# Order of the U and V gathers in the expert stage of a decoder layer: blocks of 16 in place of alternation

## The chip, the cores and the metric

The kernel runs on one core of a Trainium2 chip. The metric is the device time of one execution in microseconds (us), less is better; the numbers given are medians of runs. The profile is one execution taken by the hardware profiler. Its engines: PE (TensorE, matrix multiply), DVE (VectorE), ACT (ScalarE), POOL (GpSimd) and SP (SyncE), each with its own in-order instruction stream, and 16 DMA engines that move data between HBM and on-chip memory.

## What is computed

A decoder layer for 256 tokens of width 2048 in float32: attention and short convolution, output projection, LayerNorm, then product-key experts (PEER), LayerNorm. The change touches only the experts:

```python
def _peer(h, w_query, sub_keys, expert_u, expert_v):
    ...
    eid = i1 * N_KEYS + i2                    # 16 experts of 16384 per token and head
    g = jax.nn.softmax(best_s, axis=-1).astype(h.dtype)
    ...
    def chunk(args):
        hx, e, gw = args
        a = jax.nn.gelu(jnp.einsum('td,thkd->thk', hx, expert_u[e]))
        return jnp.einsum('thk,thkd->td', gw * a, expert_v[e])
```

There are 8 heads and 16 experts a head. Each expert is one row of 2048 floats in `expert_u` and one in `expert_v`, so every token needs 128 rows of each: 256 x 128 x 2 rows of 8 KB, 512 MiB in all.

## The kernel before

The first third, up to about 634 us, is projections, attention and the query scores. The expert stage follows. It is cut into 16 units (`NU`): unit n is one head for one tile of 128 tokens (units 0 to 7 are tile 0, 8 to 15 tile 1). A unit has 16 expert places k (`TOPK`). For each (n, k) there is one U gather and one V gather: an indirect DMA that POOL issues and that fetches 128 rows (one for each token of the tile) of 8 KB, 1 MiB in all. U(n,k) and V(n,k) stand for them below; m = 16n + k.

- POOL (L351 to L377) issues all gathers from one in-order stream. `gather_u` waits at k = 0 for the ids of the unit (`ids_ok`), and always for a free place in the ring of 8 U tiles (`RU`): `dots_done` of m - 8. `gather_v` waits for a free place in the ring of 8 V tiles (`RV`): `v_used` of m - 8. All gathers go to one DMA queue. At the start all of U(0,.) is issued; then the loop over n pairs U(n+1,k) with V(n,k).
- DVE (from L1251) makes `ids(0)`, the top-k that gives `eid`. Then for each unit it does 16 times `dot(n,k)` (L1217), which multiplies a U tile with the token tile `xh` and sums along the row. Behind dot 0 of a unit stands `gates_of(n-1)` (L1220), behind dot 1 `ids(n+1)` (L1163 to L1210), and behind dot 2 of unit 9 `take(0)` (L1229), which adds the finished sum of tile 0 to `xh` and takes its statistics; it waits until all 128 V tiles of tile 0 are used.
- ACT turns the 16 dots of a unit into Gelu values (L865) and, once the gates are there, writes 16 diagonal matrices 128x128 (L872) in one of two halves of `diag`.
- PE (L625) multiplies each diagonal with the V tile (four products of 128x512, each of which is two rows in the profile: 8 rows a V tile), summing a whole token tile's 128 experts in four PSUM banks. Its V tiles come in the order of m. It waits for `diag_ok` at the start of a unit, for the landing of each V tile, and before unit 8 for `acc_taken` of `take(0)`.
- SP loads the two rows of the last LayerNorm once all ids are there, and stores the output.

The order of the work is written by hand; no scheduler moves it.

Of the kernel before, what the change touches and what calls it, by code (L numbers as in the profile page):

```python
# [29 lines left out]
TOPK = 16  # L30
# [22 lines left out]
def build(nc, x, w_in, cmp_k_pos, cmp_k_w1, cmp_k_b1, cmp_k_w2, cmp_v_pos, cmp_v_w1, cmp_v_b1, cmp_v_w2,  # L53
# [248 lines left out]
    def _(pool):  # L302
# [48 lines left out]
        def gather_u(n, k):  # L351

            m = TOPK * n + k
            if k == 0:
                pool.wait_ge(S["ids_ok"], n + 1)
            if m >= RU:
                pool.wait_ge(S["dots_done"], m - RU + 1)
            nc.gpsimd.indirect_dma_start(out=u_slot[m % RU][:, :], out_offset=None, in_=expert_u[0],  # L358
                                         in_offset=bass.IndirectOffsetOnAxis(ap=eid[:, n, k:k + 1], axis=0)
                                         ).then_inc(s_u[m % RU], 16)  # L360

        def gather_v(n, k):

            m = TOPK * n + k
            if m >= RV:
                pool.wait_ge(S["v_used"], m - RV + 1)
            nc.gpsimd.indirect_dma_start(out=v_slot[m % RV][:, :], out_offset=None, in_=expert_v[0],  # L367
                                         in_offset=bass.IndirectOffsetOnAxis(ap=eid[:, n, k:k + 1], axis=0)
                                         ).then_inc(s_v[m % RV], 16)
# [3 lines left out]
        for n in range(NU):  # L373
            for k in range(TOPK):
                if n + 1 < NU:
                    gather_u(n + 1, k)
                gather_v(n, k)  # L377


# [913 lines left out]
```

## Time and profile before

| what | value |
|---|---|
| median of 3 runs | 1963.75 us (1963.17 to 1964.27) |
| the profiled execution, whole | 1962.15 us |
| its span | 1960.4 us |
| expert stage | about 634 to 1946 us |
| PE busy over the span | 1548.9 us, 79% |
| DVE busy | 1092.1 us, 56% |
| POOL busy | 700.9 us, 36% |
| HBM traffic | 328 GB/s over the span, 421 in the expert stage |

How to read it: the page cuts the span into 40 slices of 49 us and gives for each the busy share in tenths, the granted clock of PE (1.00 is 2.4 GHz, 0.50 is 1.2 GHz), the mean share of the 16 DMA engines and what they moved. A window row has first the window and its length, then the busy time and the number of instructions of PE, PE's weight loads, DVE, ACT and POOL, and at its end the granted clock, the DMA share and GB/s. A row of the timeline has start, duration, engine, line, operation and operands, and in brackets how long the engine was idle before it and what ended that. A row of the chain has start, duration and what the time went to.

### The profile page before, as it was taken

Reading aid. Unit: us, or ns where it says so; the run is one execution under the profiler, and the core shown is the slowest. Engines: PE = TensorE matmul, PEld = TensorE weight load, DVE = VectorE, ACT = ScalarE, POOL = GpSimd, SP = SyncE. Lnnn points to the kernel's source line nnn. Section 1 sums busy time; section 2 is a strip of 40 time slices with the busy share of each in tenths; the row PEclk is TensorE's granted clock in tenths of the full one; section 3 lists DMA queues with packets and bytes.
Section 4 is the critical chain, followed back from the end, with each engine's and each line's share of the span. In section 5 each row is a group of like instructions: output and inputs, shape, how many; then the busy total and the mean of one; then the engine's idle time right before and its main releaser. Section 6 shows DMA issues by size and latency. Waiting matters only on the chain.

```text
span 1960.4 us, 18229 instructions
## 1 busy us (share of the span) xinstructions
PE 1548.9 (79%) x6469; PEld 935.4 (48%) x6469; DVE 1092.1 (56%) x1775; ACT 446.0 (23%) x918; POOL 700.9 (36%) x562
## 2 busy tenths in 40 slices
PE   6999999999897077776877767775877687776886
PEld 6679989989897033232322323322333232232333
DVE  3666656655744866465564655647646466454432
ACT  3655465464443011011010110101101001010010
POOL 1100000000000784554655546554555554545420
PEclk8899999999898589989999999997999999989999
DMA  9555444445541999999999999999999999999992
GB/s 305 204 193 153 145 135 152 147 133 178 163 155 47 416 421 421 422 422 422 422 421 422 422 422 422 421 422 422 421 422 421 421 422 421 422 422 421 422 407 104
DMA packets 172979, 644.59 MB, mean 329 GB/s; under 512 B 13310, under 2 KB 100454, under 8 KB 106856
## 3 DMA queue, kind: packets, MB, share of 16 engines
q0 software_dynamic: 78640, 556.83, 68.8%
q1 hardware_dynamic: 90976, 85.99, 14.0%
q10 hardware_dynamic: 3288, 0.78, 0.2%
q8 instruction: 46, 0.75, 0.2%
q14 instruction: 29, 0.24, 0.0%
HBM read 641.46 MB, written 2.10 MB: 328 GB/s over the span
## 4 chain that ended last, share of the span: by engine, by line
DMA 49%; PE 37%; POOL 5%; DVE 4%; issue 2%; ACT 1%; DVEq 1%; ACTq 1%; POOLq 0%
DMA v_slot<-in_expert_v_dram,eid 41%; PE psum_all L404 21%; PE psum_all L625 9%; DMA u_slot<-in_expert_u_dram,eid 8%; POOL u_slot L358 3%; POOL v_slot L367 2%; PE psum_all L520 1%; DVE u_slot L1217 1%; PE psum_all L456 1%; PE psum_all L457 1%; PE psum_all L458 1%; ACT diag L872 1%; DVE w_lo L902 1%; PE psum_all L594 0%; ACTq L645 0%
## 5 line engine op out<-in xcount | busy, mean ns | idle before, releaser
L625 PE MATMUL psum_all<-v_slot,diag 128*128 128x512 f32 x2048 | 959.9, 620 | 361.8 <-DMA v_slot<-in_expert_v_dram,eid 188.4
L1217 DVE SCALAR_TENSOR_TENSOR u_slot<-u_slot,xh 128x2048 f32<-128x2048 f32 x256 | 583.4, 2291 | 518.6 <-DMA u_slot<-in_expert_u_dram,eid 518.4
L625 PEld LDWEIGHTS psum_all<-v_slot,diag 128*128 128x128 f32 x2048 | 388.5, 197 | 932.6 <-issue 448.5
L367 POOL DMA_INDIRECT v_slot<-in_expert_v_dram,eid x256 | 386.6, 1510 | 514.8 <-PE psum_all L625 478.2
L358 POOL DMA_INDIRECT u_slot<-in_expert_u_dram,eid x256 | 295.9, 1156 | 212.5 <-DVE eid L1210 124.5
L902 DVE TENSOR_TENSOR w_lo<-w_ring,w_hi 128x512 fp32r<-128x512 f32 x304 | 205.8, 690 | 176.1 <-ACT w_hi L656 173.5
L404 PE MATMUL psum_all<-act_hi,w_hi 128*128 128x256 f32 x896 | 260.6, 291 | 14.5 <-DVE w_lo L902 13.6
L404 PE MATMUL psum_all<-act_hi,w_lo 128*128 128x256 f32 x896 | 256.0, 286 | 0.0
L404 PE MATMUL psum_all<-act_lo,w_hi 128*128 128x256 f32 x896 | 256.0, 286 | 0.0
L656 ACT ACTIVATE w_hi<-w_ring 128x512 fp32r<-128x512 f32 x304 | 189.0, 629 | 184.4 <-PE psum_all L404 184.2
L865 ACT ACTIVATE u_act<-u_dot 128x16 f32<-128x16 f32 x16 | 3.4, 215 | 932.0 <-DVE u_slot L1217 932.0
L404 PEld LDWEIGHTS psum_all<-act_hi,w_hi 128*128 128x128 f32 x896 | 174.7, 195 | 19.0 <-DVE act_lo L907 10.3
L404 PEld LDWEIGHTS psum_all<-act_lo,w_hi 128*128 128x128 f32 x896 | 174.8, 195 | 0.5 <-issue 0.5
L404 PEld LDWEIGHTS psum_all<-act_hi,w_lo 128*128 128x128 f32 x896 | 174.4, 195 | 0.0
L349 POOL DMA_DIRECT2D skeys<-in_sub_keys_dram x1 | 1.2, 1172 | 393.9 <-PE psum_all L404 393.9
L872 ACT ACTIVATE diag<-ident,gate 128x128 f32<-128x128 f32 x256 | 76.5, 387 | 75.3 <-DVE gate L1226 75.3
L404 PE MATMUL psum_all<-w_hi,mix_hi 128*128 128x256 f32 x256 | 74.0, 289 | 0.0
L404 PE MATMUL psum_all<-w_lo,mix_hi 128*128 128x256 f32 x256 | 73.4, 287 | 0.0
L404 PE MATMUL psum_all<-w_hi,mix_lo 128*128 128x256 f32 x256 | 73.3, 286 | 0.0
L404 PEld LDWEIGHTS psum_all<-w_hi,mix_hi 128*128 128x128 f32 x256 | 50.1, 196 | 0.7 <-issue 0.7
L404 PEld LDWEIGHTS psum_all<-w_lo,mix_hi 128*128 128x128 f32 x256 | 50.1, 196 | 0.3 <-issue 0.3
L404 PEld LDWEIGHTS psum_all<-w_hi,mix_lo 128*128 128x128 f32 x256 | 50.1, 196 | 0.0
(201 smaller groups left out, 969.3 us busy)
## 6 DMA issues: line engine op xcount, KB each, us to landing
w_ring<-in_w_in_dram SPq DMA_DIRECT2D x88, 512.0 KB, 4.7
w_ring<-in_w_out_dram SPq DMA_DIRECT2D x32, 512.0 KB, 4.5
w_ring<-in_w_query_dram SPq DMA_DIRECT2D x32, 512.0 KB, 4.5
w_ring<-in_cmp_k_w_dram POOLq DMA_DIRECT2D x8, 1024.0 KB, 7.1
w_ring<-in_cmp_v_w_dram POOLq DMA_DIRECT2D x8, 1024.0 KB, 5.7
u_slot<-in_expert_u_dram,eid POOLq DMA_INDIRECT x256, 36.3
v_slot<-in_expert_v_dram,eid POOLq DMA_INDIRECT x256, 35.7
xh<-in_x_dram SPq DMA_DIRECT2D x4, 512.0 KB, 7.4
```

The lines of the kernel that those rows point to most:

```text
L358: nc.gpsimd.indirect_dma_start(out=u_slot[m % RU][:, :], out_offset=None, in_=expert_u[0], in_offset=bass.IndirectOffsetOnAxis(ap=eid[:, n ...
L367: nc.gpsimd.indirect_dma_start(out=v_slot[m % RV][:, :], out_offset=None, in_=expert_v[0], in_offset=bass.IndirectOffsetOnAxis(ap=eid[:, n ...
L404: ins = nc.tensor.matmul(o, st, mv, start=(k == 0 and b == 0 and n == 0), stop=(k == KC - 1 and n == 2), skip_group_check=True)
L456: nc.tensor.matmul(o, blk_hi[:, kv, j, :], w_hi[:, q % 4, :], start=(j == 0), stop=False)
L457: nc.tensor.matmul(o, blk_hi[:, kv, j, :], w_lo[:, q % 4, :], start=False, stop=False)
L458: nc.tensor.matmul(o, blk_lo[:, kv, j, :], w_hi[:, q % 4, :], start=False, stop=False).then_inc(S["slot_used"], 1)
L520: ins = nc.tensor.matmul(bank[6][:, 128 * t:128 * t + 128], vv, pp, start=(n == 0), stop=(n == len(parts) - 1))
L625: ins = nc.tensor.matmul(bank[4 + q][:, :], diag[:, n % 2, k, :], v_slot[m % RV][:, 512 * q:512 * q + 512], start=m % (TOPK * PH) == 0, st ...
L656: nc.scalar.activation(w_hi[:, q % 4, :], src, ACT.Copy).then_inc(S["hi_done"], 1)
L872: ins = nc.scalar.activation(diag[:, n % 2, k, :], ident[:, :], ACT.Copy, scale=gate[:, n, k:k + 1])
L902: V.tensor_tensor(w_lo[:, q % 4, :], src, w_hi[:, q % 4, :].bitcast(F32), ALU.subtract).then_inc(S["lo_done"], 1)
L1217: V.scalar_tensor_tensor(u_slot[m % RU][:, :], u_slot[m % RU][:, :], 1.0, xh[:, n // PH, :], ALU.mult, ALU.mult, accum_out=u_dot[:, n, k:k ...
```

## The change

In the loop over units POOL issued U(n+1,k) and V(n,k) in turn. Now it issues the 16 U gathers of unit n+1 first and then the 16 V gathers of unit n. Waits, rings and slots stay as they were, and so does every other engine's program.

```diff
         for n in range(NU):
             for k in range(TOPK):
                 if n + 1 < NU:
                     gather_u(n + 1, k)
+            for k in range(TOPK):
                 gather_v(n, k)
```

On POOL, where the gathers of V(0,.) end and those of U(2,.) begin, the program stands so before; `u_slot0` with both waits is U(2,0), the V rows ahead of it are V(0,12) to V(0,15):

```order
L358 DMA u_slot4_143<-in_expert_u_dram,eid_126 128x2048 [waits dots_done]
L367 DMA v_slot4_151<-in_expert_v_dram,eid_126 128x2048 [waits v_used]
L358 DMA u_slot5_144<-in_expert_u_dram,eid_126 128x2048 [waits dots_done]
L367 DMA v_slot5_152<-in_expert_v_dram,eid_126 128x2048 [waits v_used]
L358 DMA u_slot6_145<-in_expert_u_dram,eid_126 128x2048 [waits dots_done]
L367 DMA v_slot6_153<-in_expert_v_dram,eid_126 128x2048 [waits v_used]
L358 DMA u_slot7_146<-in_expert_u_dram,eid_126 128x2048 [waits dots_done]
L367 DMA v_slot7_154<-in_expert_v_dram,eid_126 128x2048 [waits v_used]
L358 DMA u_slot0_139<-in_expert_u_dram,eid_126 128x2048 [waits dots_done,ids_ok]
L367 DMA v_slot0_147<-in_expert_v_dram,eid_126 128x2048 [waits v_used]
```

The same engine and place after:

```order
L367 DMA v_slot4_151<-in_expert_v_dram,eid_126 128x2048 [waits v_used]
L367 DMA v_slot5_152<-in_expert_v_dram,eid_126 128x2048 [waits v_used]
L367 DMA v_slot6_153<-in_expert_v_dram,eid_126 128x2048 [waits v_used]
L367 DMA v_slot7_154<-in_expert_v_dram,eid_126 128x2048 [waits v_used]
L358 DMA u_slot0_139<-in_expert_u_dram,eid_126 128x2048 [waits dots_done,ids_ok]
L358 DMA u_slot1_140<-in_expert_u_dram,eid_126 128x2048 [waits dots_done]
L358 DMA u_slot2_141<-in_expert_u_dram,eid_126 128x2048 [waits dots_done]
L358 DMA u_slot3_142<-in_expert_u_dram,eid_126 128x2048 [waits dots_done]
L358 DMA u_slot4_143<-in_expert_u_dram,eid_126 128x2048 [waits dots_done]
L358 DMA u_slot5_144<-in_expert_u_dram,eid_126 128x2048 [waits dots_done]
```

All of U(1,.) has moved ahead of V(0,.), and each wait for `v_used` now stands ahead of 16 U gathers instead of one.

On POOL at the end of the U gathers, before (the last U here is U(15,15), beside it V(14,15), and V(15,.) follows):

```order
L358 DMA u_slot6_145<-in_expert_u_dram,eid_126 128x2048 [waits dots_done]
L367 DMA v_slot6_153<-in_expert_v_dram,eid_126 128x2048 [waits v_used]
L358 DMA u_slot7_146<-in_expert_u_dram,eid_126 128x2048 [waits dots_done]
L367 DMA v_slot7_154<-in_expert_v_dram,eid_126 128x2048 [waits v_used]
L367 DMA v_slot0_147<-in_expert_v_dram,eid_126 128x2048 [waits v_used]
L367 DMA v_slot1_148<-in_expert_v_dram,eid_126 128x2048 [waits v_used]
L367 DMA v_slot2_149<-in_expert_v_dram,eid_126 128x2048 [waits v_used]
```

The same end of U(15,.) after:

```order
L358 DMA u_slot4_143<-in_expert_u_dram,eid_126 128x2048 [waits dots_done]
L358 DMA u_slot5_144<-in_expert_u_dram,eid_126 128x2048 [waits dots_done]
L358 DMA u_slot6_145<-in_expert_u_dram,eid_126 128x2048 [waits dots_done]
L358 DMA u_slot7_146<-in_expert_u_dram,eid_126 128x2048 [waits dots_done]
L367 DMA v_slot0_147<-in_expert_v_dram,eid_126 128x2048 [waits v_used]
L367 DMA v_slot1_148<-in_expert_v_dram,eid_126 128x2048 [waits v_used]
L367 DMA v_slot2_149<-in_expert_v_dram,eid_126 128x2048 [waits v_used]
L367 DMA v_slot3_150<-in_expert_v_dram,eid_126 128x2048 [waits v_used]
```

Behind the last U gather 32 V gathers are left, where 17 were.

## Rows read from the trace of the kernel before

**Rows 1.** The page: DMA share and GB/s in 40 slices; the chain by line.
```profile
DMA  9555444445541999999999999999999999999992
GB/s 305 204 193 153 145 135 152 147 133 178 163 155 47 416 421 421 422 422 422 422 421 422 422 422 422 421 422 422 421 422 421 421 422 421 422 422 421 422 407 104
...
DMA v_slot<-in_expert_v_dram,eid 41%; PE psum_all L404 21%; PE psum_all L625 9%; DMA u_slot<-in_expert_u_dram,eid 8%; POOL u_slot L358 3%; POOL v_slot L367 2%; PE psum_all L520 1%; DVE u_slot L1217 1%; PE psum_all L456 1%; PE psum_all L457 1%; PE psum_all L458 1%; ACT diag L872 1%; DVE w_lo L902 1%; PE psum_all L594 0%; ACTq L645 0%
```

**Rows 2.** Window row of one unit (columns as told above).
```profile
1158.60:1239.00 80.40, 60.16 (x128) 24.04 (x128) 45.03 (x69) 7.91 (x21) 42.19 (x33) 0.96 1.01 421
```

**Rows 3.** Timeline in the steady part of a unit: DVE, POOL, PE, POOL.
```profile
1146.28 2.29 DVE L1217 SCALAR_TENSOR_TENSOR u_slot<-u_slot,xh 128x2048 f32<-128x2048 f32 x1 [2.66 <-DMA u_slot<-in_expert_u_dram,eid]
...
1147.78 1.59 POOL L367 DMA_INDIRECT v_slot<-in_expert_v_dram,eid  x1 [2.12 <-PE psum_all L625]
...
1148.78 3.70 PE L625 MATMUL psum_all<-v_slot,diag 128*128 128x512 f32 x8 [1.28 <-DMA v_slot<-in_expert_v_dram,eid]
...
1149.68 0.94 POOL L358 DMA_INDIRECT u_slot<-in_expert_u_dram,eid  x1 [0.30 <-issue]
...
1151.24 2.29 DVE L1217 SCALAR_TENSOR_TENSOR u_slot<-u_slot,xh 128x2048 f32<-128x2048 f32 x1 [2.67 <-DMA u_slot<-in_expert_u_dram,eid]
```

**Rows 4.** Timeline of ACT: the Gelu row of unit 1 and of unit 15.
```profile
759.50 0.22 ACT L865 ACTIVATE u_act<-u_dot 128x16 f32<-128x16 f32 x1 [57.69 <-DVE u_slot L1217]
...
1885.01 0.21 ACT L865 ACTIVATE u_act<-u_dot 128x16 f32<-128x16 f32 x1 [69.31 <-DVE u_slot L1217]
```

**Rows 5.** The page's DMA issues: count, median us from issue to landing.
```profile
u_slot<-in_expert_u_dram,eid POOLq DMA_INDIRECT x256, 36.3
```

**Rows 6.** The chain of the last 80 us.
```profile
1882.67 2.31 DVE u_slot L1217 x2
...
1885.61 4.79 ACT diag L872 x16
...
1890.44 55.22 PE psum_all L625 x128
```

**Rows 7.** Startup gathers issued at 634.2, 635.5, 648.1 and 657.3: time to landing.
```profile
DMA to landing us min/median/max: 5.4/5.4/5.4
...
DMA to landing us min/median/max: 7.9/7.9/7.9
...
DMA to landing us min/median/max: 15.2/15.2/15.2
...
DMA to landing us min/median/max: 8.5/8.5/8.5
```

**Rows 8.** Timeline of DVE: first row of unit 1's top-k, dot 2 behind it.
```profile
690.87 0.48 DVE L1168 MAX8 t_val<-scores 128x8 f32<-128x128 f32 x2
...
699.99 2.29 DVE L1217 SCALAR_TENSOR_TENSOR u_slot<-u_slot,xh 128x2048 f32<-128x2048 f32 x1
```

**Rows 9.** Timeline of POOL while DVE does dots back to back.
```profile
669.18 1.91 POOL L358 DMA_INDIRECT u_slot<-in_expert_u_dram,eid  x1 [0.30 <-issue]
```

**Rows 10.** Window rows of the startup's U stream.
```profile
650.00:670.00 20.00, 0.00 (x0) 0.00 (x0) 19.41 (x28) 1.68 (x3) 11.20 (x6) 0.50 1.01 413
...
660.00:670.00 10.00, 0.00 (x0) 0.00 (x0) 10.00 (x9) 0.00 (x0) 8.47 (x6) 0.50 1.00 400
...
670.00:672.00 2.00, 0.00 (x0) 0.00 (x0) 2.00 (x3) 0.00 (x0) 1.70 (x2) 0.50 1.04 430
```

**Rows 11.** Timeline of DVE: `take(0)` from its first row to the dot behind it.
```profile
1340.68 2.48 DVE L1234 SCALAR_TENSOR_TENSOR xh<-xh,psum_all 128x512 f32<-128x512 f32 x4
...
1346.17 2.29 DVE L1217 SCALAR_TENSOR_TENSOR u_slot<-u_slot,xh 128x2048 f32<-128x2048 f32 x1
```

**Rows 12.** PE's clock behind idle time: window rows, and PE's row at 1343.
```profile
1168.70:1172.50 3.80, 3.76 (x5) 1.69 (x6) 3.43 (x20) 1.28 (x1) 0.00 (x0) 0.50 1.01 423
...
1343.26 50.02 PE L625 MATMUL psum_all<-v_slot,diag 128*128 128x512 f32 x112 [19.79 <-DVE xh L1234]
...
1347.00:1352.00 5.00, 5.00 (x13) 2.18 (x12) 5.00 (x5) 0.00 (x0) 2.78 (x2) 1.00 1.01 421
```

## Prediction

> **What bounds the kernel now.** I read the slices and the chain of the page first [rows 1]. From slice 14 on (about 637 us) the DMA digit is 9 and 421 to 422 GB/s flow in every slice until the last two. That is the expert stage: 512 gathers of 1 MiB. The chain is mostly `v_slot` and `u_slot` DMA. One unit (16 U and 16 V gathers) takes 80.4 us, DMA share 1.01, and in it PE is busy 60.2 us, DVE 45.0 and POOL 42.2 [rows 2]: three engines with room, and DMA with none. U gathers are 4.97 us apart in the steady part [rows 3], so a gather of either kind costs 2.49 us of DMA; over all units it is (1885.01 - 759.50)/14 = 80.4 us a unit [rows 4], 80.0 without the two LayerNorm rows, which take about 5 us of DMA once. In [rows 3] DVE waits 2.67 us for each U, PE 1.26 us for each V, and POOL for PE: about 14 gathers stand in the DMA queue, which is why one takes 36 us to land [rows 5]. Nothing but the rate of DMA sets the unit. The end is different [rows 6]: after the last U gather (landed 1882.67) come its dots, the gates, 4.79 us of diagonals, and then 55.2 us in which PE works through unit 15's 16 V tiles, 3.45 us each, while DMA runs dry; then 14.7 us of final LayerNorm and store to the span's 1960.4.
>
> **What the change moves.** No instruction is added or removed; POOL's 480 paired gathers are put in blocks, with the same waits. The total of DMA work is the same 512 x 2.49 us. What can change is whether the queue ever runs empty, and what is left for after its end.
>
> Term 1, the end. Before, U(15,15) is gather number 16 + 14x32 + 31 = 495 in POOL's order. After, all U of unit 15 come first, then V(14) and V(15): V(14,0) is number 16 + 14x32 + 16 + 1 = 481. If DMA never idles it lands 14 x 2.49 = 34.9 us before 1882.67, at 1847.8. From there PE has 32 V tiles in one run, as V comes at 2.49 us and PE needs 3.45: 2.1 us of slow start (below) + 32 x 3.45 = 112.5 us, to 1960.3, where it now ends at 1945.65. That is **+14.7 us**, and certain as long as DMA sets the pace before it: in the alternating order half of that PE work lay under U transfers. The gates of unit 15 (5 us of diagonals) leave the path; that is inside the sum.
>
> Term 2, the steady unit. Does a block order keep DMA full? Follow POOL from the issue of V(n-1,15), t = 0. U(n+1,0) is issued 0.94 + 0.30 us later [rows 3]; behind one other gather it lands 7.9 us after its issue [rows 7]: t = 9.1. DVE then does dot 0 (2.21, the pitch of back-to-back dots [rows 9]), the gates (0.75, an estimate for two small instructions) and dot 1 (2.21) and starts the top-k of the next unit, from 690.87 to 699.99 = 9.1 us [rows 8]: 23.4. No further U slot comes free in that time. Six more dots at 2.21 (13.3) free the slot of U(n+1,15): 36.7. While dots run back to back POOL issues one gather per dot, 1.91 + 0.30 = 2.21 us [rows 9], so U(.,15) and V(n,0) are out at 41.1. DMA by then has 18 gathers to do since t = 0: V(n,0) lands near 18 x 2.49 + 2.9 = 47.7 (2.9 = 5.4 for a lone gather [rows 7] less its own 2.49). PE has been idle some 20 us and starts slow; then 8 V tiles (2.1 + 8 x 3.45 = 29.7) must be used before V(n,15) may be issued: t = 77.4. The unit of DMA is 80.0, so this loop fits with 2.6 us to spare, one gather's worth. Likeliest is therefore no loss, but a margin of 3% replaces a queue of 14 gathers.
>
> The tighter spot inside the unit is the top-k. The first ten U are in flight when it starts; the eleventh waits for dot 2, 2.21+0.75+2.21+9.1+2.21+0.35 = 16.8 us after U(.,0) landed, and the ninth further gather lands 9 x 2.49 = 22.4 us after it. An issue of up to 2.74 us under a dot and 4.4 us from there to landing end at 24.0 against the 24.9 us at which an unbroken stream would deliver it: 0.9 us to spare. The startup of the present trace is this very case, since its first 16 gathers are U alone. The tenth, issued at 648.1, landed at 663.3; the eleventh, issued at 657.3, at 665.8 [rows 7]: 2.5 us later, so no gap; and DMA moved 413 GB/s between 650 and 670 [rows 10] against 421 in a steady unit [rows 2] (2% less). By the first number the cost is nothing, by the second 2% of the 40 us of U in each unit, 0.8 us, over 14 units 11 us. I take 0.2 us a unit, **+3 us** (bounds 0 and +11), nearer to the landing times, since the sequel has V gathers left in the queue which the startup had not.
>
> The Trainium skill (SBUF — State Buffer, the paragraph on DVE blocking software-generated DMA) says GpSimd can be locked out by a DVE instruction and the DMA engines then sit idle for want of descriptors. Taken whole, it would idle DMA for much of each block of 16 dots (35 us a unit, 490 us in all); the trace shows the lockout only as the 2.21 us pitch, and DMA busy through it, so the sum takes nothing for it. The skill (DMA: Bandwidth & Descriptors, Anatomy of one DMA) fits 2.0 us + bytes/436 GB/s, 4.4 us for 1 MiB; the lone gather here took 5.4 with its issue. With 4.4 the loop would end at 76.4 in place of 77.4 and change nothing.
>
> Term 3, two places where DVE is late. At the start DVE runs behind (its first top-k stands in unit 0's dots), so unit 1's top-k at 690.87 to 699.99 falls when only U(1,0..9) may be out. U(1,0) landed at 681.1, U(1,9) would by 703.5; U(1,10) waits for dot 2, is issued at 702.5 and lands some 7.9 later, 710.4, where an unbroken stream has 706.0. Now V gathers fill this hole. **+3 us** (2 to 4.4). And `take(0)` stands behind dot 2 of unit 9: 1340.68 to 1346.17, 5.5 us of DVE [rows 11], plus up to 2 us in which it waits for V(7)'s last tile. Now 14 queued gathers hide it; after, it is in the loop above, where it meets 1 to 2.6 us of room: **+4.5 us** (3 to 6.5).
>
> Term 4, PE's clock. PE falls to a granted 0.50 in idle time and stays there 3.8 us after it starts [rows 12]: a matmul, 3.45/8 = 0.43 us at full clock, takes twice that, and about 2.1 us are lost. This happens once a unit now (6.3 us idle) and once a unit after (idle 80 - 57 = 23 us); the start after 19.8 us of idle is no longer than after 6.3. It is in the loop already.
>
> Sum: 14.7 + 3 + 3 + 4.5 = **+25 us**. On the profiled span of 1960.4 that is 1985.6. The execution profiled took 1962.15 in all, and the median of the three is 1963.75; I add to the median: **1989 us**, 1.3% slower.
>
> **Rivals.**
> - *Stretched unit.* The 2.6 us margin is not there, say because queued gathers land later than I take it or PE's slow start lasts twice as long (4.2 us): each unit is then 2 to 4.5 us over 80. For it: two spots with under 3 us to spare, and 400 GB/s between 660 and 670 in the startup's U stream [rows 10]. Against: the landing times. Price: 14 x 2 to 14 x 4.5 on top of 25: 2017 to 2052, middle about 2030.
> - *Shallow queue is slower.* DMA needs more than some 2 gathers in flight for its rate. With those 400 GB/s instead of 421, the 1245 us stream grows 5%, 62 us: 2051.
> - *Not slower.* A stream from one table goes faster than one that alternates. The startup's U stream has moments of 430 GB/s (670 to 672) [rows 10]; if the blocks held that, 2.1% of 1245 us = 26 us come back: 1963, and it decides from there: only above 430 GB/s is the kernel faster. Against: the 20 us around it have 413. The skill (DMA: Bandwidth & Descriptors) gives a ceiling of about 436 GB/s, which would be 3.5%, 44 us, and a time near 1945; no row here sustains it.
> - *No block in effect.* If rings kept U and V in lockstep anyway, nothing would change (1964). They can't: POOL is in order, and V(n,0) stands behind U(n+1,15).
>
> **Chances.** Forecast (DMA-bound units, +12 to +40): 0.66. Stretched unit: 0.20. Slower shallow queue, or several of these together (over +70): 0.06. Not slower or in effect nothing: 0.08, of it 0.03 faster by over 0.2%. 0.2% (4 us) is about what a measurement of this kernel can tell from no change. The range must hold 8 in 10: it begins at term 1 alone less 3 us, +12, and reaches into the stretched unit, 3.5 us a unit, +66: 1976 to 2030.
>
> **What would show it.** After: units of 80 us still, by the distance of the Gelu rows; DMA at 9 in all slices of the stage, with a dip near 705 and 1350; PE in runs of about 57 us with some 23 us between; the last PE run about 112 us, starting near 1858. Diagonals no longer end PE's idle time; the first V of a block does. Landing of gathers falls from 36 to some 10 us. Units of 82 us or more, or DMA slices of 7 and 8, would show the margin gone; under 80 us, a faster stream. I am wrong in kind if PE's last run stays near 55 us.

## The result and the profile after

The changed kernel takes **1992.49 us** (median of 4 runs, 1991.3 to 1993.92) against 1963.46 us of the kernel before in the same measurement: ratio 1.0152, 95% interval 1.0135 to 1.017, so 29 us slower. The forecast was 1989 us, the range 1976 to 2030. The profiled execution has a span of 1989.7 us, 29.3 more than before.

The page after, with the same two rows of slices and the same row of the chain as [rows 1], and the gathers' time to landing as in [rows 5]:

```profile
DMA  9555445445452999999999999999999999999992
GB/s 301 203 189 164 134 138 164 135 141 185 141 169 92 421 374 411 422 420 421 416 419 412 417 414 419 414 422 368 422 421 415 421 421 410 422 421 413 422 342 102
...
PE psum_all L626 26%; PE psum_all L405 21%; POOL u_slot L358 9%; DMA v_slot<-in_expert_v_dram,eid 8%; DVE u_slot L1218 6%; DMA u_slot<-in_expert_u_dram,eid 6%; POOL v_slot L367 1%; PE psum_all L521 1%; PE psum_all L457 1%; PE psum_all L459 1%; PE psum_all L458 1%; DVE w_lo L903 1%; DVE eq L1201 1%; DVE b_id L1209 1%; DVE t_idx L1179 0%
...
u_slot<-in_expert_u_dram,eid POOLq DMA_INDIRECT x256, 12.9
v_slot<-in_expert_v_dram,eid POOLq DMA_INDIRECT x256, 10.7
```

The line numbers from L380 on are one higher than before. Read the two rows of slices together. The DMA digit is 9 in every slice of the stage, as before; by it alone nothing happened. The GB/s row shows what did: 374 in slice 15, 368 in slice 28, 410 to 419 in many others where before stood 421 and 422, and 342 in the last but one, where before stood 407. The chain has turned over. Where DMA of `v_slot` held 41%, it now holds 8%, and the product of PE (L626) went from 9 to 26%. Gathers land after 11 to 13 us where they took 36: the queue that hid everything is short.

PE's runs after, from its timeline: the V tiles of unit 0, of unit 6, of units 7 and 8 (between them `take(0)`), of unit 13, and of 14 and 15 in one:

```profile
726.12 56.94 PE L626 MATMUL psum_all<-v_slot,diag 128*128 128x512 f32 x128 [102.13 <-DMA v_slot<-in_expert_v_dram,eid]
...
1209.36 57.66 PE L626 MATMUL psum_all<-v_slot,diag 128*128 128x512 f32 x128 [23.28 <-DMA v_slot<-in_expert_v_dram,eid]
...
1289.97 56.61 PE L626 MATMUL psum_all<-v_slot,diag 128*128 128x512 f32 x128 [22.95 <-DMA v_slot<-in_expert_v_dram,eid]
1375.38 56.58 PE L626 MATMUL psum_all<-v_slot,diag 128*128 128x512 f32 x128 [28.80 <-DMA v_slot<-in_expert_v_dram,eid]
...
1782.49 57.81 PE L626 MATMUL psum_all<-v_slot,diag 128*128 128x512 f32 x128 [27.72 <-DMA v_slot<-in_expert_v_dram,eid]
1863.41 111.55 PE L626 MATMUL psum_all<-v_slot,diag 128*128 128x512 f32 x256 [23.11 <-DMA v_slot<-in_expert_v_dram,eid]
```

A unit's 16 V tiles are one unbroken run of 57 us behind 23 us of idle time, and the diagonals no longer end that idle time. The last row is term 1 of the prediction: 256 rows, 32 tiles, 111.55 us, where [rows 6] had 128 rows and 55.22.

The windows of the three other places, after. The columns are those of [rows 2]; the last three are granted clock, DMA share, GB/s.

```profile
704.00:714.00 10.00, 0.00 (x0) 0.00 (x0) 10.00 (x11) 0.00 (x0) 8.72 (x5) 0.50 0.82 301
1173.00:1213.00 40.00, 16.72 (x36) 7.12 (x35) 39.04 (x64) 6.53 (x17) 24.79 (x14) 0.72 1.00 407
1300.00:1360.00 60.00, 46.59 (x109) 20.33 (x107) 28.23 (x59) 7.75 (x20) 20.63 (x20) 0.92 0.93 383
```

The same windows before:

```profile
704.00:714.00 10.00, 10.00 (x25) 4.38 (x24) 6.59 (x7) 0.00 (x0) 8.48 (x6) 1.00 1.02 423
1173.00:1213.00 40.00, 33.64 (x76) 13.47 (x74) 23.30 (x30) 1.68 (x3) 24.54 (x18) 1.00 1.01 422
1300.00:1360.00 60.00, 35.11 (x75) 14.46 (x76) 40.78 (x70) 7.96 (x21) 23.94 (x17) 0.83 1.01 422
```

The first is the hole of the start, the third that of `take(0)`, and the second the dip behind the top-k of an ordinary unit. There the DMA share is 1.00 (1.01 before) while 4% fewer bytes come. The strip of DMA over 1133 to 1213, 2 us a column, shows where in the unit:

```profile
GB/s 410 426 418 426 426 422 426 414 426 414 426 422 426 422 422 422 406 434 414 434 418 414 422 418 422 418 426 397 307 401 348 356 426 414 438 414 442 410 442 410
```

Columns 28 to 32 (1187 to 1197 us) fall to 307 to 401. The top-k of this unit ran from 1173.95 to 1182.9, and the next U gather behind it was issued at 1185.48. The same strip over 1293 to 1373, with `take(0)` in it, falls to nothing:

```profile
GB/s 430 410 434 418 422 422 422 430 406 434 414 434 410 426 426 410 438 406 430 414 430 410 418 434 410 434 414 426 414 381 74 0 94 414 406 393 320 377 422 426
```

### The profile page after: what moved, and what is told of

The parts are those of the page before. It is cut to its first block, busy times and chain, and to the rows that moved or that the text cites. A ratio compares the mean times of both kernels' runs of the same rounds, so it can differ in the third digit from the quotient of the medians.

```text
span 1989.7 us, 18229 instructions
## 1 busy us (share of the span) xinstructions
PE 1501.4 (75%) x6469; PEld 945.9 (48%) x6469; DVE 1077.1 (54%) x1775; ACT 445.8 (22%) x918; POOL 746.3 (38%) x562
## 4 chain that ended last, share of the span: by engine, by line
PE 53%; DMA 14%; DVE 14%; POOL 11%; issue 5%; DVEq 2%; ACT 1%; ACTq 1%; POOLq 0%
PE psum_all L626 26%; PE psum_all L405 21%; POOL u_slot L358 9%; DMA v_slot<-in_expert_v_dram,eid 8%; DVE u_slot L1218 6%; DMA u_slot<-in_expert_u_dram,eid 6%; POOL v_slot L367 1%; PE psum_all L521 1%; PE psum_all L457 1%; PE psum_all L459 1%; PE psum_all L458 1%; DVE w_lo L903 1%; DVE eq L1201 1%; DVE b_id L1209 1%; DVE t_idx L1179 0%
## 5 line engine op out<-in xcount | busy, mean ns | idle before, releaser
L626 PE MATMUL psum_all<-v_slot,diag 128*128 128x512 f32 x2048 | 912.7, 609 | 438.3 <-DMA v_slot<-in_expert_v_dram,eid 438.3
L626 PEld LDWEIGHTS psum_all<-v_slot,diag 128*128 128x128 f32 x2048 | 399.7, 196 | 950.6 <-issue 950.6
L1218 DVE SCALAR_TENSOR_TENSOR u_slot<-u_slot,xh 128x2048 f32<-128x2048 f32 x256 | 571.2, 2286 | 510.6 <-DMA u_slot<-in_expert_u_dram,eid 510.4
L358 POOL DMA_INDIRECT u_slot<-in_expert_u_dram,eid x256 | 383.4, 1498 | 372.5 <-DVE u_slot L1218 171.8
L367 POOL DMA_INDIRECT v_slot<-in_expert_v_dram,eid x256 | 344.5, 1346 | 339.3 <-PE psum_all L626 284.3
L405 PE MATMUL psum_all<-act_hi,w_hi 128*128 128x256 f32 x896 | 260.8, 291 | 14.7 <-DVE w_lo L903 12.2
L1235 DVE SCALAR_TENSOR_TENSOR xh<-xh,psum_all 128x512 f32<-128x512 f32 x8 | 5.0, 681 | 105.9 <-PE psum_all L626 105.9
```

The costliest lines, as they stand in the source:

```text
L405: ins = nc.tensor.matmul(o, st, mv, start=(k == 0 and b == 0 and n == 0), stop=(k == KC - 1 and n == 2), skip_group_check=True)
L626: ins = nc.tensor.matmul(bank[4 + q][:, :], diag[:, n % 2, k, :], v_slot[m % RV][:, 512 * q:512 * q + 512], start=m % (TOPK * PH) == 0, st ...
L1218: V.scalar_tensor_tensor(u_slot[m % RU][:, :], u_slot[m % RU][:, :], 1.0, xh[:, n // PH, :], ALU.mult, ALU.mult, accum_out=u_dot[:, n, k:k ...
```

## The experiments

Each run is compared with the kernel before in the same measurement. That kernel's median was 1963.46 us when the change was measured and 1959.99, 1962.51 and 1960.79 in the three later measurements, so a difference between two kernels that were not measured together can be off by up to 3.5 us; where it matters, the difference of the two losses, each against its own kernel before, stands beside it ("by the losses"). In the texts of expectation "theory" and "rival" are the two readings that the run is to tell apart. The first theory ("end and holes") is the prediction's: the loss is a longer end and three kinds of holes in which DVE is late. Its rival: a stream in blocks is slower as such, by a short queue or by reading one table at a time.

### Undoing the end, and the end alone

The lines that are new against the changed kernel (the four in the middle stand as there, further in):

```diff
+            if n + 1 < NU - 1:           # first run; in the second: if n + 1 == NU - 1
                 for k in range(TOPK):
                     gather_u(n + 1, k)
                 for k in range(TOPK):
                     gather_v(n, k)
+            else:
+                for k in range(TOPK):
+                    if n + 1 < NU:
+                        gather_u(n + 1, k)
+                    gather_v(n, k)
```

> The changed kernel with the last pair alone, U(15) with V(14), put back into alternation; units before it stay in blocks. Theory 'end and holes': the last U gather is number 495 of the order again, so PE's last run is 55 us and the 14.7 us of term 1 go: 1992.5 - 14.7 = 1978 us. Rival 'slower stream' (the loss is spread over all block units because a stream in blocks moves fewer GB/s): one unit of 15 is mended, about 2 us: 1990 us.

Measured: 1976.73 us against 1959.99, ratio 1.0076 (1.0059 to 1.0093).

> The kernel before with the last pair alone, U(15) and V(14), in blocks. Theory 'end and holes': only term 1, 1963.5 + 14.7 = 1978 us, last PE run about 112 us, units of 80.0 us up to there. Rival 'slower stream': one unit of 15, 1965 us.

Measured: 1974.26 us against 1959.99, ratio 1.0074 (1.0053 to 1.0095), +14.3 us for one reordered pair. Its last PE run:

```profile
1846.40 111.85 PE L631 MATMUL psum_all<-v_slot,diag 128*128 128x512 f32 x256 [38.62 <-DMA v_slot<-in_expert_v_dram,eid]
```

Term 1 said 14.7 us. It is there when only the last pair is in blocks, and it goes when only the last pair is put back: the median falls by 15.8 us, and the loss against the kernel before of each measurement from 29.0 to 16.7, by 12.3. A rate of the stream would have given 2 us in either.

### Moving DVE's long pieces behind dot 8

```diff
-                if k == 1 and n + 1 < NU:
+                if k == 8 and n + 1 < NU:
                     ids(n + 1)
-                if k == 2 and n == PH + 1:
+                if k == 8 and n == PH + 1:
                     take(0)
```

The last U gather of a block waits for dot 7, so behind dot 8 neither piece holds up a gather.

> The changed kernel with the top-k of the next unit behind dot 8 in place of dot 1, and take(0) behind dot 8 of unit 9 in place of dot 2; all U gathers of a block can then be issued without waiting for either. Theory 'end and holes': the dips of DMA behind the top-k, the hole at 704 to 714 us and the hole of take(0) go, 14 to 15 us; the end stays: 1978 us, units of 80.0 us. Rival 'slower stream' (some 10 gathers in flight in place of 14, or one table at a time, is what costs): nothing depends on DVE's order: 1990 to 1992 us.

Measured: 1977.76 us against 1959.99, ratio 1.0085 (1.0066 to 1.0103), 14.7 us less than the changed kernel (11.3 by the losses, 29.0 and 17.8). The profiled spans, 1989.7 and 1975.2, differ by 14.5. The same three windows:

```profile
704.00:714.00 10.00, 0.00 (x0) 0.00 (x0) 9.38 (x33) 0.00 (x0) 7.87 (x8) 0.50 1.01 422
1173.00:1213.00 40.00, 17.29 (x34) 7.28 (x33) 33.32 (x59) 1.90 (x4) 20.77 (x15) 0.70 1.01 422
1300.00:1360.00 60.00, 39.26 (x92) 17.10 (x90) 35.31 (x65) 7.75 (x20) 35.96 (x28) 0.86 1.01 420
```

301, 407 and 383 GB/s have become 422, 422 and 420. Over whole slices small dips are left (410 to 422). The U gathers still come in blocks of 16 from one table.

> Blocks in units 0 to 13, last pair in alternation, and top-k and take(0) behind dot 8: both edits of the two runs beside it together. Theory 'end and holes': nothing of the loss is left, 1963 to 1966 us, though 13 of 15 pairs are still in blocks. Rival 'slower stream': 1988 us or more.

Measured: 1962.4 us (10 runs) against 1959.99 (13), ratio 1.0009 (0.9999 to 1.002). With 14 of 15 pairs in blocks (the expectation says 13; it is 14) 2.4 us are left of 29, and the interval holds no change as well as a loss of 3.9. This settles the first question: block order as such costs at most 0.2%, and the rival, which asked for 1988 us or more, falls. Whether the 2 us are real is open. By PE's starts an ordinary unit of this run takes 80.2 us; in the kernel before it is 80.0 by the Gelu rows.

With the top-k alone moved:

> The changed kernel with only the top-k moved behind dot 8; take(0) stays behind dot 2 of unit 9. Theory 'end and holes': the start's hole (3 us) and the dips in the units (5 to 7 us) go, that of take(0) (4.5 us) stays, so of the 14.7 us which both moves gave back 9 to 10 come from the top-k: 1982 to 1983 us. If take(0) were the larger part, 1988 us.

Measured: 1985.52 us against 1962.51, ratio 1.0126 (1.0109 to 1.0143): 7.0 us less than the changed kernel (6.0 by the losses), not 9 to 10. So `take(0)` is about half of the two moves' gain, more than I gave it.

From PE's rows the shares can be read one by one, as the distance between the starts of its runs in the changed kernel and in the run with both pieces moved. The first run starts at 726.12 and 720.72: the start's hole is 5.4 us. From the run at 1289.97 to that at 1375.38 it is 85.4 us, with both moved 79.5: `take(0)` costs 5.9. All other units together (726.12 to 1289.97 and 1375.38 to 1863.41 against the same pieces there, 561.8 and 486.2) cost 2.0 + 1.8 = 3.8. The run with both moved still has the long end: its last PE run ends at 1960.37, 14.7 us behind the 1945.65 of before. These are single executions. The run with only the last pair put back has the same order up to unit 13 as the changed kernel, and its PE starts span 2.5 us more there, so the 3.8 is good to about 2 us.

### How much room the loop had

The prediction's loop runs from V(n-1,15) to V(n,15) and was to leave 2.6 us of 80. One V tile less makes it 3.45 us longer and changes nothing for DMA.

```diff
-RV = 8
+RV = 7
```

> The changed kernel with a ring of 7 V tiles in place of 8. V(n,15) may then be issued only when nine tiles of the block are used, not eight: 3.45 us later. By the prediction's loop (77.4 us against 80.0 of DMA) the unit grows to 80.9, 14 x 0.9 = 12 us in all: 2004 us. By the trace after, in which U(n+1,0) lands 8.9 us after its issue where 7.9 is the least, only about 1 us of the margin is there: 14 x 2.4 = 34 us, 2026 us. Rival 'the loop has nothing to do with it' (holes behind the top-k alone): 1992 us.

Measured: 2036.88 us against 1962.51, ratio 1.0382 (1.0364 to 1.0399), 44 us more than with 8 tiles (45 by the losses) and more than either number. By PE's starts ordinary units take 83.7 us, where with 8 tiles they took 80.5.

> The kernel before with a ring of 7 V tiles in place of 8. Control for the run beside it: with some 13 gathers queued the unit stays DMA's 80.0 us, and the end is set by PE: no change, within 2 us of the kernel before by every theory. If the ring mattered by itself (depth of the queue as such), 5 us or more slower.

Measured: 1962.71 us (10 runs) against 1962.51, ratio 1.0002 (0.9991 to 1.0012). In alternation a ring of 7 is as good as one of 8.

So the room was not 2.6 us but almost none: the unit grew by 3.2 of the 3.45 us. The gathers at the turn from V to U in the run with 7 tiles show why. POOL's timeline, and the times to landing of these four gathers one by one:

```profile
1180.85 0.94 POOL L367 DMA_INDIRECT v_slot<-in_expert_v_dram,eid  x1 [2.50 <-PE psum_all L626]
1182.09 0.94 POOL L358 DMA_INDIRECT u_slot<-in_expert_u_dram,eid  x1 [0.30 <-issue]
1183.34 0.94 POOL L358 DMA_INDIRECT u_slot<-in_expert_u_dram,eid  x1 [0.30 <-issue]
1184.58 0.94 POOL L358 DMA_INDIRECT u_slot<-in_expert_u_dram,eid  x1 [0.31 <-issue]
```

```profile
DMA to landing us min/median/max: 5.2/5.2/5.2
DMA to landing us min/median/max: 7.5/7.5/7.5
DMA to landing us min/median/max: 8.9/8.9/8.9
DMA to landing us min/median/max: 11.4/11.4/11.4
```

They land at 1186.0, 1189.6, 1192.2 and 1196.0: 3.6, 2.6 and 3.8 us apart instead of 2.49. The V gather took 5.2 us, about the time of a lone one (5.4) [rows 7]: the queue had run down. The change of table from V to U is not needed for the wider distances, as the first two gathers of [rows 7], both U, have one too (below). From there every gather lands 2.5 us behind the one before, through the whole U block, up to V(n,0) at 1230.8. That is 50.0 us after V(n-1,15)'s issue; the prediction had 47.7. The loop is 50.0 + 2.1 + 9 x 3.45 = 83.2 us with 7 tiles. In this unit it took just that (V(n,15) was issued at 1264.06), and 83.7 us in the mean. With 8 tiles the same sum gives 79.7. In the changed kernel V(n,0) came 50.4 us behind V(n-1,15)'s issue (1158.89 to 1209.3) in the unit looked at.

Is it this, or DVE's top-k, that sets V(n,0)?

> Blocks with 7 V tiles, and the top-k and take(0) behind dot 8. With 7 V tiles the unit is 83.7 us and set by the loop from one V(n,15) to the next. Theory 'the queue sets V(n,0)': after V(n-1,15) the queue has run down to one gather, and 17 gathers at 2.49 us and two gaps of 1.1 to 1.3 us between the first landings of U bring V(n,0), whatever DVE does: the unit stays at 83 us and only the start's and take(0)'s few us go: 2028 to 2032 us. Rival 'DVE sets V(n,0)' (top-k and the dots behind it delay the last U and so V): the loop loses up to 9 us, the unit falls to 80 to 81 us: 1983 to 1995 us.

Measured: 2016.65 us, ratio 1.0279 (1.0258 to 1.0301). Neither range was met, but the first theory is the nearer: ordinary units fell only from 83.7 to 83.0 us by PE's starts. The rest of the 20 us (21.7 by the profiled spans) stands elsewhere. PE's first run starts 7.8 us earlier (720.38 for 728.16), the pair around `take(0)` is 6.1 us shorter (82.5 for 88.6), and 0.7 us in each of 12 other units makes most of the rest. I had given the first two 5 to 9 us together, and they are 14. In a unit of this run V(n-1,15) was issued at 1168.93 and V(n,0) landed at 1219.0: 50.1 us again, though POOL had issued V(n,0) 33.6 us behind V(n-1,15), where without the move it was 39.3. But for the 0.7 us a unit, DVE does not set V(n,0); the queue does.

Next, the turn itself was changed. The first four U gathers of a block were put between the last four V of the block ahead of it (the branch for the last unit, which has V gathers alone, and the ring's 7 are left out here):

```diff
+                for k in range(4 if n else 0, TOPK):
+                    gather_u(n + 1, k)
                 for k in range(TOPK):
+                    if k >= 12 and n + 2 < NU:
+                        gather_u(n + 2, k - 12)
                     gather_v(n, k)
```

> Blocks with 7 V tiles, but the first four U gathers of the next block alternate with the last four V of this one. The number of tiles in each ring and the order within U and within V stay. Theory 'loop at the block's edge': V(n,15) no longer stands ahead of the whole U block, some 10 us of the loop go and DMA is the bound again: units of 80.0 to 80.5 us, the end as in blocks: 1985 to 1993 us. Rival '7 tiles are too few for a block of 16 by themselves': 2030 us.

Measured: 1985.52 us, ratio 1.0123 (1.0107 to 1.0138). By PE's starts ordinary units are back at 79.5 to 80.7 us; only the one behind the pair with `take(0)` takes 81.5. Four gathers out of 32 moved in each unit, and 51 us came back (50 by the losses), more than the 44 to 45 that the eighth tile had been worth. Seven tiles are enough for blocks of 16 when the queue does not run down at the turn.

Last, PE's slow start. Behind units 0 to 13 PE was given 28 products that nothing uses:

```diff
                 ins.then_inc(S["v_used"], 1)
+            if n < NU - 2:
+                for _ in range(28):
+                    nc.tensor.matmul(bank[0][:, :], ident[:, :], skT[:, 0:4, :]...,
+                                     start=True, stop=True)
```

> Blocks with 7 V tiles, and behind each of units 0 to 13 PE runs 28 extra products of 128x512 into an unused bank (24.1 us of its 26 us of idle time), so that its clock is not down when V(n,0) lands. They add work that the output does not use. Theory 'loop': the 2.1 us of slow start stand in the loop, 13 x 2.1 = 27 us go: 2010 us, units 81.6 us. Rival 'PE's slow start is hidden': 2037 us as without them; more if the extra products run into V(n,0).

Measured: 2009.83 us against 1960.79, ratio 1.0239 (1.0223 to 1.0254), 27.1 us less than with 7 tiles alone (25.3 by the losses). In PE's timeline the row of 56 is the unused work, the row of 128 a unit's V tiles:

```profile
866.17 24.20 PE L632 MATMUL psum_all<-skT,ident 128*128 128x512 f32 x56
891.68 55.17 PE L626 MATMUL psum_all<-v_slot,diag 128*128 128x512 f32 x128 [1.31 <-DMA v_slot<-in_expert_v_dram,eid]
```

The V tiles take 55.17 us behind 1.3 us of idle time. The 13 runs of the changed kernel behind 23 to 29 us of idle took 57.25 on the mean (56.56 to 58.15): 2.08 us for the slow start, which is term 4's 2.1. The unused work did not remove all of it. Of the 13 runs of units 1 to 13, eight took 55.17 us, three 56.87, and the two behind some 6.7 us of idle (at `take(0)` and at the LayerNorm rows) 57.6 and 57.9. So the profiled spans' 27.3 us agree with 13 x 2.1 partly by luck: 24.5 lie between the starts of PE's first and last run, 1.4 in the last run, and 1.4 ahead of the first run, where no unused work stands. That the slow start stands in the loop is shown; that it is paid in full is not.

### Two more orders

Against the kernel before:

```diff
-            for k in range(TOPK):
-                if n + 1 < NU:
-                    gather_u(n + 1, k)
-                gather_v(n, k)
+            for k0 in (0, 8):
+                for k in range(k0, k0 + 8):
+                    if n + 1 < NU:
+                        gather_u(n + 1, k)
+                for k in range(k0, k0 + 8):
+                    gather_v(n, k)
```

> Blocks of 8 in place of 16: U(n+1,0..7), V(n,0..7), U(n+1,8..15), V(n,8..15). Theory 'end and holes': U(15,15) is number 488, 8 tiles of V(14) are left behind it, so V(14,8) lands 6 x 2.49 = 14.9 us earlier than number 495 and PE then has 24 tiles, 82.8 + 2.1 us, where before it had 63 us behind number 495: +7 us. No hole behind the top-k or take(0), as 8 V gathers stand behind the 10 U: 1967 to 1970 us. Rival 'slower stream in blocks': the loss is half or all of that of the blocks of 16, spread over the units: 1975 to 1990 us.

Measured: 1969.93 us against 1962.51, ratio 1.0045 (1.0028 to 1.0062), +7.4 us. Its last PE run is 85.64 us, its ordinary units are 79.5 to 80.6 by the Gelu rows. The end alone, by the arithmetic of term 1.

```diff
+            if n + 2 == NU:
+                gather_u(n + 1, 0)
+                gather_u(n + 1, 1)
             for k in range(TOPK):
-                if n + 1 < NU:
+                if n + 2 == NU:
+                    if k + 2 < TOPK:
+                        gather_u(n + 1, k + 2)
+                elif n + 1 < NU:
                     gather_u(n + 1, k)
                 gather_v(n, k)
```

> The kernel before, with U three places ahead of V instead of one in the last pair only: U(15,15) is number 493, V(14,13) to V(14,15) follow it. The end as computed: U(15,15) lands 2 x 2.49 = 5.0 us earlier; V(14,15) lands 7.5 us behind it and is used 3.45 later, 10.9, where the diagonals were ready at 7.8: 5.0 - 3.1 = 1.9 us faster, 0.1%: 1961 us where before has 1963, at the edge of what can be told. By the rule 'every V left behind the last U costs 0.96 us' without the diagonals' time it would be 1.9 us slower.

Measured: 1961.54 us (11 runs) against 1960.79 (15), ratio 1.0002 (0.9993 to 1.0011). The interval holds no change and just misses the 0.1% gain expected; the gain is not shown. (In the one profiled execution PE ends at 1944.03, 1.6 us earlier than before; the medians do not bear it out.) No order tried beats the kernel before.

## Why the prediction held, step by step

- **What bounds.** DMA before, at 2.49 us a gather: borne out, since putting 14 of 15 pairs in blocks costs at most 0.2% once the queue is kept filled.
- **Term 1, the end, +14.7.** 14.3 when alone (the interval allows 10 to 19), 12.3 to 15.8 when taken away, and 14.7 by the end of PE's last run when DVE's pieces are moved. PE's last run was forecast at 112.5 us and took 111.55; it was to start near 1858 and started at 1863.4, as the holes ahead of it were 5 us larger than thought.
- **Term 2, the steady unit, +3 (0 to 11).** 3.8 by PE's rows. The size is right, but the picture behind it had a term mis-sized. "18 x 2.49 + 2.9 = 47.7" left out what a queue costs that has run down: wider distances between landings at the turn, 2.4 us a unit. [rows 7] show the first of them: the gathers issued at 634.2 and 635.5 landed at 639.6 and 643.4, 3.8 us apart. The prediction used that second gather's 7.9 us to place U(n+1,0) at 9.1, and then did not count on from there: 9.1 + 16 x 2.49 is 48.9, so its own two numbers differ by 1.2 us, and it took the smaller. With the 50.0 of the trace the loop is 79.7 us, not 77.4, and the room 0.3 us, not 2.6. That the kernel lost only 3.8 us with so little room is the luck of a loop that came out just under DMA's 80.0. The rival "stretched unit" (0.20) described what one tile less in the ring did at once: 83.7 us a unit.
- **The dip behind the top-k** was placed right. Moving the top-k took it away.
- **Term 3, the start +3 and take(0) +4.5.** 5.4 and 5.9. Both undershot. The bounds were 4.4 and 6.5, so the start lay outside its own. At the start the prediction's own landing times gave 710.4 - 706.0 = 4.4, and it took 3 with no working. The sum counts only the one gather that waits, and the stream does not come back at full rate: from 709 to 716, behind the empty columns, it has 262 to 410 GB/s. Over 690 to 730 the mean is 362 GB/s, with DVE's pieces moved 422, which is 5.7 us of transfer. That the restart makes up the last 1 us is argued from these rates, not tested. For `take(0)` the trace has 5.5 us of DVE work behind 0.8 us of waiting for PE; less the 1 to 2.6 us of room the prediction came to 4.5, and less the 0.3 us that there were it would be 6.0. In the columns behind the three that are nearly empty stand 414, 406, 393, 320 and 377 GB/s.
- **Term 4, the slow start of PE, 2.1.** 2.08.
- **The sum** was 25 and is 29. By the profiled executions: 14.7 + 5.4 + 5.9 + 3.8 = 29.8, less 0.5 as the last PE run was that much shorter than in the run with DVE's pieces moved, is the 29.3 by which the spans differ. The 4 us that were missing are mostly the start's and `take(0)`'s.
- **Rivals.** "Shallow queue is slower" is refuted as a rate: with DVE's pieces moved, the three windows have 420 to 422 GB/s while a U gather lands after 15.7 us and a V gather after 13.4 in the median, where before it was 36. "Not slower", that one table at a time streams faster than 421, is refuted by the same rows. The Trainium skill (SBUF — State Buffer, the paragraph on DVE blocking software-generated DMA) says that GpSimd is locked out and the DMA engines sit idle while DVE runs an operation in a two-port mode. No run here shows whether the dots are such operations. What the trace shows under them is POOL's 1.91 us in place of 0.94 for a gather, and in the run with DVE's pieces moved the row of 1173 to 1213, with DVE busy 33 of 40 us and 422 GB/s, speaks against a cost of it here.

## What to carry to other kernels

In a stage that one queue feeds, two streams with different consumers can be put in blocks at little or no loss (here at most 0.2%) as long as the queue never runs down; so write out the loop of waits from one block's last issue to the next one's and compare it with the time the queue needs for a block. The room in it is what counts, and it can be measured by taking one buffer away, which makes the loop longer by one step of the consumer (here 3.45 us): no effect means at least that much room, an effect of the full step means there is none. The end is a sum of its own: whatever the slower consumer has left when the other stream is through is exposed, here 0.96 us (3.45 - 2.49) for each further V tile left behind, and the last block should be ordered for that alone.

## What the runs showed of the hardware

- The share of busy DMA engines is 1.00 while the rate falls by 4% over 40 us (407 against 422 GB/s), and in 2 us columns down to 307. A queue that runs thin showed in GB/s and not in the page's digit; the share of a window fell clearly only where the queue ran empty (0.82 and 0.93).
- A queue that has run down to one gather lands some of the next ones further apart than the 2.49 us of an unbroken one: 3.6, 2.6 and 3.8 us with 7 V tiles, and 3.8 us between the first two of the stage [rows 7]. What in the engines takes this time was not tried.
- PE's slow start costs 2.08 us in the mean of 13 runs behind 23 to 29 us of idle time, and no more (56.94 - 55.17 = 1.8 us) behind 102 us. The granted clock of a start is the lower level, 1.2 GHz, as in [rows 12].
